# Attention probabilities turned by VectorE and a DRAM round trip instead of by TensorE; background DRAM sums started every tenth unit throughout

## The reference

```python
xn = rms_norm(h, norm_mix_g)
proj = xn @ w_in                     # q, k, v of both mixers
# mixer A: 16 query heads, 4 key heads, window of the current and the previous 64-token chunk, ALiBi, sinks
# mixer B: 16 heads, the current and all earlier chunks, learned relative-position bias
sc = q @ k.T * (dh ** -0.5) + bias   # masked by chunk
p = softmax(sc)                      # the probabilities
att = p @ v
y_a, y_b = att_a @ w_branch_a, att_b @ w_branch_b
gates = sigmoid(xn @ w_gate)
h = h + (gates[:, :D] * y_a + gates[:, D:] * y_b) @ w_out
u = square(relu(rms_norm(h, norm_mlp_g) @ w_mlp_in))
h = h + u @ w_mlp_out
out = rms_norm(h, norm_final_g)
```

## Time and profile before

| | |
|---|---|
| median of 3 runs | 2479.81 us (2479.39 to 2479.84) |
| the profiled execution's own time | 2479.84 us |
| its span | 2477.9 us |
| TensorE busy | 2460.3 us, 99% of the span |
| VectorE busy | 1658.9 us, 67% |
| ScalarE busy | 1062.5 us, 43% |
| GpSimd busy | 193.2 us, 8% |
| DMA queue q1 (hardware, SP's) | 364.04 MB |
| DMA queue q0 (software, POOL's) | 151.00 MB |
| mean granted TensorE clock | 0.998 of full speed |

### The profile page before, as it was taken

The page is one execution under the profiler, slowest core; times in us unless marked ns, Lnnn a source line. Parts: engine busy times, 40 slices in busy tenths (PEclk is TensorE's granted clock), DMA queues, the critical chain, the costliest instruction groups (busy, mean ns, idle before and its releaser), DMA issues.

```text
span 2477.9 us, 34645 instructions
## 1 busy us (share of the span) xinstructions
PE 2460.3 (99%) x14162; PEld 2176.5 (88%) x14162; DVE 1658.9 (67%) x2252; ACT 1062.5 (43%) x1381; POOL 193.2 (8%) x185
## 2 busy tenths in 40 slices
PE   9999999999999999999999999999999999999998
PEld 8898898898888888888999999999998888888886
DVE  6566555556333332544788888888869788877897
ACT  5566755556222222312433433333335444444445
POOL 0010100100010100001200000000001011110010
PEclk9999999999999999999999999999999999999999
DMA  7789998898889999964564433334478666566652
GB/s 261 208 236 261 240 246 243 233 253 225 227 241 271 245 254 254 251 184 151 167 192 152 136 129 132 133 128 132 133 233 332 232 230 226 190 224 231 233 191 107
DMA packets 226818, 517.10 MB, mean 209 GB/s; under 512 B 30672, under 2 KB 159840, under 8 KB 215152
## 3 DMA queue, kind: packets, MB, share of 16 engines
q1 hardware_dynamic: 213856, 364.04, 44.3%
q0 software_dynamic: 12672, 151.00, 24.1%
q10 hardware_dynamic: 144, 0.02, 0.0%
HBM read 489.80 MB, written 176.20 MB: 269 GB/s over the span
## 4 chain that ended last, share of the span: by engine, by line
PE 96%; DVE 2%; ACT 1%; DMA 0%; issue 0%; SPq 0%; DVEq 0%; ACTq 0%
PE bank L1707 31%; PE bank L1709 31%; PE bank L1708 31%; PE bank L1782 1%; PE bank L1817 1%; PE bank L1796 1%; DMA stream<-in_x_features 0%; DVE up_lo L1398 0%; DVE form_lo_b L1364 0%; DVE at_lo L1248 0%; ACT q_twice L742 0%; DVE ring L1506 0%; ACT w_hi L686 0%; ACT L714 0%; DVE raw_forms L1469 0%
## 5 line engine op out<-in xcount | busy, mean ns | idle before, releaser
L1032 DVE TENSOR_TENSOR w_lo<-landing,w_hi 128x1024 fp32r<-128x1024 f32 x199 | 247.6, 1244 | 447.2 <-ACT w_hi L686 447.1
L1707 PE MATMUL bank<-xn_hi,w_hi 128*128 128x512 f32 x1184 | 464.7, 392 | 2.3 <-DVE w_lo L1189 1.4
L1709 PE MATMUL bank<-xn_hi,w_lo 128*128 128x512 f32 x1184 | 461.2, 390 | 0.0
L1708 PE MATMUL bank<-xn_lo,w_hi 128*128 128x512 f32 x1184 | 460.8, 389 | 0.0
L686 ACT ACTIVATE w_hi<-landing 128x1024 fp32r<-128x1024 f32 x199 | 210.9, 1060 | 575.6 <-PE bank L1709 575.2
L909 ACT ACTIVATE up_hi<-up_raw 128x1792 fp32r<-128x1792 f32 x128 | 218.1, 1704 | 401.8 <-PE bank L1709 395.0
L958 ACT ACTIVATE ring<-down_raw 128x1024 fp32r<-128x1024 f32 x224 | 237.5, 1061 | 312.4 <-PE bank L1709 312.4
L1506 DVE TENSOR_TENSOR ring<-down_raw,ring 128x1024 fp32r<-128x1024 f32 x224 | 284.9, 1281 | 68.3 <-ACT ring L958 68.2
L1398 DVE TENSOR_TENSOR up_lo<-up_raw,up_hi 128x1792 fp32r<-128x1792 f32 x128 | 259.8, 2030 | 85.8 <-ACT up_hi L909 85.8
L1707 PEld LDWEIGHTS bank<-xn_hi,w_hi 128*128 128x128 f32 x1184 | 222.4, 188 | 47.3 <-issue 3.3
L1709 PEld LDWEIGHTS bank<-xn_hi,w_lo 128*128 128x128 f32 x1184 | 222.2, 188 | 46.9
(11 more groups left out here) (192 smaller groups left out, 4384.1 us busy)
## 6 DMA issues: line engine op xcount, KB each, us to landing
down_totals<-in_down_blocks POOLq DMA_DIRECT2D x64, 1024.0 KB, 9.5
up_raw<-in_up_units SPq DMA_DIRECT2D x128, 512.0 KB, 3.4
down_raw<-down_totals SPq DMA_DIRECT2D x128, 512.0 KB, 4.4
down_raw<-in_down_blocks SPq DMA_DIRECT2D x96, 512.0 KB, 4.3
landing<-in_w_in SPq DMA_DIRECT2D x71, 512.0 KB, 6.5
landing<-in_w_gate SPq DMA_DIRECT2D x64, 512.0 KB, 6.5
landing<-in_w_out SPq DMA_DIRECT2D x32, 512.0 KB, 3.7
hidden_rows<-hidden_out SPq DMA_DIRECT2D x32, 512.0 KB, 3.3
```

What stands on the lines that cost most here:

```text
L1032: nc.vector.tensor_tensor(w_lo[:, s, :], landing[:, u % LAND, :], w_hi[:, s, :].bitcast(F32), ALU.subtract).then_inc(unit_lo, 1)
L1707: nc.tensor.matmul(dst, a_hi, b_hi, start=start, stop=False, **kw)
L1708: nc.tensor.matmul(dst, a_hi, b_lo, start=False, stop=False, **kw)
L1709: return nc.tensor.matmul(dst, a_lo, b_hi, start=False, stop=stop, **kw)
```

## The change

The transposes on TensorE are gone. DVE now transposes each 128x128 block of probabilities in 32x32 squares (`turn_probs`, into `probs_by_block`), right behind the normalisation of the same head. A DMA stores that to DRAM (`store_probs`: 448 KB for a head of A, 640 KB for one of B), and four DMAs of 32 partitions each bring it back with the squares in their places (`load_probs`, into `pt_raw`), so that keys lie on the partitions. ACT and DVE split `pt_raw` in one instruction each. `TURN_AT` is now three units behind the scores and `PV_AT` four; the last six heads' scores are two units apart. PE's scores of the next head wait for the bias addition of the head before, not for `pt_lo`. For mixer A, v is multiplied with whole 128-query blocks (256 columns where there were 192). SP stores and loads for heads 0 to 30, POOL for head 31, in front of set 7. A set of DRAM sums now starts at 12, 20 and then 18 + 10m: set 17 at 188.

```diff
-SCORES_AT = [13 + 2 * k for k in range(16)] + [46, 48, 51, 53, 56, 59, 62, 65, 68, 71, 74, 76, 78, 81, 83, 85]
-TURN_AT = [n + 1 for n in SCORES_AT]
-PV_AT = [n + 2 for n in SCORES_AT]
-PV_AT[28] = 81
+SCORES_AT = [13 + 2 * k for k in range(16)] + [46, 48, 51, 53, 56, 59, 62, 65, 68, 71, 74, 76, 78, 80, 82, 84]
+TURN_AT = [n + 3 for n in SCORES_AT[:-1]] + [SCORES_AT[-1] + 2]
+PV_AT = [n + 4 for n in SCORES_AT[:-1]] + [SCORES_AT[-1] + 3]
...
+        def store_probs(queue, h, out):
+            queue.wait_ge(probs_turned, h + 1)
+            if h >= 2:
+                queue.wait_ge(turned_back, 64 * (h - 1))
+            size = turned_size(h)
+            queue.dma_start(turned_probs[h % 2, :, 0:size], probs_by_block[:, 0:size]).then_inc(out, 16)
+
+        def load_probs(queue, h, out, landed, back):
+            queue.wait_ge(out, landed)
+            if h:
+                queue.wait_ge(pv_done, h)
+            size = turned_size(h)
+            for r in range(4):
+                rows = slice(32 * r, 32 * (r + 1))
+                cols = slice(r * size // 4, (r + 1) * size // 4)
+                src = turned_probs[h % 2, :, cols].rearrange("(a c) n -> c a n", c=32)
+                queue.dma_start(pt_raw[rows, 0:size].rearrange("p (a n) -> p a n", a=4), src)\
+                    .then_inc(back, 16)
...
+                    if n - 6 in SCORES_AT:
+                        store_probs(sp, SCORES_AT.index(n - 6), turned_out)
+                    if n - 7 in SCORES_AT:
+                        h = SCORES_AT.index(n - 7)
+                        load_probs(sp, h, turned_out, 16 * (h + 1), turned_back)
...
+            def turned_high(h):
+                if h < HEADS - 1:
+                    act.wait_ge(turned_back, 64 * (h + 1))
+                else:
+                    act.wait_ge(last_back, 64)
+                size = turned_size(h)
+                nc.scalar.activation(pt_hi[:, 0:size], pt_raw[:, 0:size], ACT.Copy).then_inc(pt_hi_done, 1)
...
+            def turn_probs(h):
+                dve.wait_ge(probs_ready, TT * (h + 1))
...
+                for k, (t, j) in enumerate(blocks):
...
+                    ins = nc.vector.transpose(out[:, k], probs[:, start:start + P])
+                ins.then_inc(probs_turned, 1)
...
             for m in range(2 + STEPS):
-                pool.wait_ge(unit_used, 12 + 8 * m if m < 10 else 84 + 10 * (m - 9))
+                if m == 7:
+                    store_probs(pool, HEADS - 1, last_out)
+                    load_probs(pool, HEADS - 1, last_out, 16, last_back)
+                pool.wait_ge(unit_used, 12 + 8 * m if m < 2 else 18 + 10 * m)
                 for part in range(6):
                     totals(m, part)
             form_sums()
...
                 if h:
-                    pe.wait_ge(pt_lo_done, TT * h)
+                    pe.wait_ge(biased, TT * h)
...
-            def turn_probs(h):
...
-                        ins = nc.tensor.transpose(bank[:, bk, col + k * P:col + (k + 1) * P],
-                                                  probs[:, start + k * P:start + (k + 1) * P], identity[:])
...
-                pe.wait_ge(pt_lo_done, TT * (h + 1))
+                pe.wait_ge(pt_lo_done, h + 1)
```

More of the change, by code:

```diff
@@ L133, in turned_keys, with turned_blocks @@
     return P * (1 + (t > 0)) if h < A_HEADS else P * (t + 1)
-def bank_end(h, t):
-    tiles = head_tiles(h)
-    return max(i for i in range(TT) if tiles[i][2] == tiles[t][2]) + 1
+def turned_blocks(h):
+    if h < A_HEADS:
+        return [(t, j) for j in range(TT) for t in (j, j + 1) if t < TT]
+    return [(t, j) for j in range(TT) for t in range(j, TT)]
 PV_BANK = 7
@@ L201, in build @@
         prologue.close()
+        raw_probs = ExitStack()
+        sb("raw_probs_pad", [P, 24 * SEQ + PROBS], F32, raw_probs)
+        pt_raw = sb("pt_raw", [P, PROBS], F32, raw_probs)
+        raw_probs.close()
         first_phase = ExitStack()
@@ L1161, in normalise, with turned_low @@
                                             ALU.mult).then_inc(probs_ready, 1)
-            def turned_probs(h):
-                for t, (first, n, bk, col, _) in enumerate(head_tiles(h)):
-                    dve.wait_ge(pt_hi_done, TT * h + bank_end(h, t))
-                    turned = bank[:, bk, col:col + turned_keys(h, t)]
-                    if h < A_HEADS:
-                        turned = turned.rearrange("p (b n) -> p b n", n=P)
-                    nc.vector.tensor_tensor(turned_part(pt_lo, h, t), turned, turned_part(pt_hi, h, t).bitcast(F32),
-                                            ALU.subtract)\
-                        .then_inc(pt_lo_done, 1)
+            def turn_probs(h):
+                dve.wait_ge(probs_ready, TT * (h + 1))
+                if h == 0:
+                    dve.wait_ge(unseen_zero, 1)
+                else:
+                    dve.wait_ge(turned_out, 16 * h)
+                blocks = turned_blocks(h)
+                out = probs_by_block[:, 0:turned_size(h)].rearrange("p (r b j) -> p b r j", r=4, j=32)
+                for k, (t, j) in enumerate(blocks):
+                    _, n, _, _, at = head_tiles(h)[t]
+                    start = at + n - turned_keys(h, t) + P * (j if h >= A_HEADS else j - max(t - 1, 0))
+                    ins = nc.vector.transpose(out[:, k], probs[:, start:start + P])
+                ins.then_inc(probs_turned, 1)
+            def turned_low(h):
+                dve.wait_ge(pt_hi_done, h + 1)
+                size = turned_size(h)
+                nc.vector.tensor_tensor(pt_lo[:, 0:size], pt_raw[:, 0:size], pt_hi[:, 0:size].bitcast(F32),
+                                        ALU.subtract).then_inc(pt_lo_done, 1)
             nc.vector.memset(ones, 1.0).then_inc(ones_ready, 1)
@@ L1227, in _ @@
                 if m in TURN_AT:
[L1228 removed]
+                    turned_low(TURN_AT.index(m))
                 if m in PV_AT:
@@ L1232, in _ @@
                     normalise(head)
+                    turn_probs(head)
                 if m % KU == KU - 1:
```

66 lines of the change are left out of this document (25 added, 41 removed).

## The result

| | before | after |
|---|---|---|
| median | 2479.62 us (2479.39 to 2479.84) | 2599.64 us (2596.28 to 2608.28, 4 runs) |
| ratio | 1 | 1.0488 (95% interval 1.0475 to 1.0502) |
| profiled span | 2477.9 us | 2606.4 us |

The account below looks back on a forecast made before the run. PE, busy 99% of the span, was taken as the bound. -31.5 + 1.5 + 27 + 7.5 + 4 + 13 = +21.5 us on 2479.84 gave 2501, less a little for overlapping waits 2499 us; range 2474 to 2532.

Parts of the forecast that it names:

- The transposes: PE, 16 heads of each mixer: the removed transposes save 31.5 us.
- wider products: Mixer A's products with v on PE, 256 instead of 192 columns: 1.5 us more, at most 2.8.
- The last set: Output projection: set 17 delays form_sums on GpSimd, so ACT's form_high(0) and then PE wait; +27 us, 19 to 33.
- T: The moment PE has finished 188 units, put at 1143.6 us, when set 17 now starts.
- Head 31: Its store and loads on GpSimd's queue make PE's last product with v late; +7.5 us, 3 to 14.
- ACT's window: First phase: ACT's time before PE's next scores shrinks, so seven mixer A heads wait; +4 us, 0 to 6.
- Late round trips: First phase: store and load of probabilities land too late for ACT's copy, PE waits; +13 us, 0 to 50.
- Rival (b): Round trip bounds the first phase, landings of 9 to 11 us cost some 50 us; about 2535 us, chance 0.19.

Follow-up runs that it names:

- the run with a first phase of 590.0: Changed kernel with all DRAM sums moved behind unit 88 and ACT's copy of pt_raw ahead of the exponentials; 2561.25 us.
- the run with the schedule alone: Kernel before with only the start of the DRAM sums changed (from set 2 on at 18 + 10m units, the last at 188); 2510.13 us.
- The best variant: Changed kernel, trips one unit longer (heads 0-25 but 15), loads before next store, pt_raw's own place in mixer A, 4 KB rows (sets 0-7), ACT's copy first; 2538.19 us.
- the idle trips: Kernel before plus unread stores and loads for heads 0 to 20, each head loading what the previous stored (0 and 16 their own); 2480.03 us.

## Why the prediction was wrong

- **The transposes, -31.5, and wider products, +1.5**: together right within some 2 us, by the run with a first phase of 590.0. The moving operand in pieces of 32 costs nothing visible; products of 256 columns follow one another by 0.12 us at the full clock.
- **The last set, +27 (19 to 33)**: the mechanism right to the line, the size 34. Set 17 took 52.3 us from first to last issue where I took 46.5. The sentence "set 16 ends before T in any case" was wrong: set 17 left right behind set 16, with no idle time between (POOL's timeline above), some 3 us behind T (estimate: T is 1143.6 - 599.1 us behind the start of the branches). In the run with the schedule alone it was the same, so the trips have no part in it.
- **Head 31, +7.5, and ACT's window, +4**: PE waited 5.7 for the last product, in size. For queries it waited 11.7 (10.5 for ACT's copies), above the bound of 6; the run with a first phase of 590.0, its trips in time, still has 7.1 there (4.8 for ACT, 2.3 for DVE), so this term was too small even apart from late trips.
- **Late round trips, +13 (0 to 50): the step that failed.** PE was idle 71 us in front of products with v, and 94.4 + 31.5 - 1.5 - 88.3 = 36 us more of the first phase are work at the lower clock by subtraction; 32.6 us of it are seen directly, in PE's busy time against the run with a first phase of 590.0. Of the 71 us some 10 are not lateness: six waits of 1.4 to 1.8 us in mixer B are those of ACT's exponentials ahead of its copy, which the step left out at heads three units apart; in the runs without sums in the first phase that order alone was worth 24.5 us (614.5 to 590.0). The rest are late trips, and three parts of that step were wrong. The sizes: I took 6.5 and 6.5 us, and 8 in mixer B, from a trace whose SP queue had no trips in it; with them the store alone took 10.3 and the weights 10.8 beside the sums. The rule "every chain spans two heads, half of that is lost per head, heads three units apart lose nothing": load(h) waits on SP for store(h)'s landing and for PE's product of h-1, and store(h+1) stands behind load(h). So trips hardly overlap (in the head shown, 3 us of a load's landing beside the next store), and the lateness is paid at each head in full: 17.1 us from store to store, 17.3 from product to product, not 12.7. And the price of waiting: I left the clock out because no row showed it.
- **Rival (b)** had the right mechanism and about half the size: 50 us for 71 of waiting and some 36 of clock. It halved the loss per head as well, and it had no clock.
- The Trainium skill on the clock ("TensorE: Matmul & The Clock Gate", section "What's actually happening": it halves after idleness and recovers under work) is borne out here: after the waits at 150 us the granted clock was 0.62 and 0.67 for 10 us, that is partly 1.2 instead of 2.4 GHz, and a matmul of 512 columns took 0.68 us instead of 0.39. I named that rule and gave it no term; at 33 to 36 us it was worth more than twice the 13 us that I gave the trips.

What stays open: which of the two row lengths, 64 or 8 KB, made the landings late, and whether the trips would fit in full with two buffers in mixer B, which no run tried (in mixer A the second buffer gained nothing, 661.3 against 660.3). The best variant's first phase is 32 us longer than 590.0: 24 us of idle PE (44.8 against 21.1) and 9 us of longer matmuls. Its largest waits are 16.6 us for products with v, 12.7 for the last of them behind GpSimd's queue, and 11.4 for queries.

## What to carry to other kernels

Where a transfer is put between two instructions, count the whole loop (issue, landing, the next issue's waits, landing, use) against the time between two rounds, with landings read beside the heaviest traffic and not beside today's. If one buffer or one in-order queue closes the loop, all lateness is paid every round. Then ask what else the idle engine loses: here 88 us of waits on TensorE, each of 10 us or less, went with 33 to 36 us more at the lower clock.

## What the runs showed of the hardware

- With sums in DRAM running (100 to 200 us), landings depend on the sums' row length: copies in rows of 64 KB and accumulations in rows of 8 KB gave 10.8 us for a 512 KB load of weights and 10.3 for a 448 KB store; with 4 KB for both it was 6.6 and 7.8, at a higher DMA share (0.99 instead of 0.90) and rate (261 instead of 251 GB/s). Without sums the store took 2.5.
- A DMA share of 0.90 and 244 GB/s before was not the limit: the idle trips ran at 1.05 and 295 GB/s, with PE whole, though a load of weights then landed in 11.7 us instead of 6.5.
- The same matmuls of the first phase (3140 in the trace) kept PE busy 568.9 us at a mean granted clock of 0.99 and 601.5 us at 0.93.
- A store on ACT's own queue landed no sooner (10.8 us) than on SP's shared one (10.3).
